# State space heads: logarithms of the time steps in the exponent, masks written by GpSimd

## The reference, cut to what matters

```python
def segsum_exp(a):                     # a = dt * A, T = 128
    cs = jnp.cumsum(a, axis=-1)
    diff = cs[..., :, None] - cs[..., None, :]
    tri = np.tril(np.ones((T, T), dtype=bool))
    return jnp.where(tri, jnp.exp(jnp.where(tri, diff, 0.0)), 0.0)
...
xdt = x * dt
CB = einsum('bclgn,bcsgn->bcgls', Cc, Bc)
Wd = CB * segsum_exp(adt)
y_diag = einsum('bcgrls,bcsgrp->bclgrp', Wd, xdt)
```

## Time and profile before

| | |
|---|---|
| median of 3 runs | 1833.98 us (1832.61 to 1834.04) |
| span of the profiled execution | 1831.0 us |
| PE busy | 1790.9 us, 98% |
| DVE busy | 1178.2 us, 64% |
| ACT busy | 846.6 us, 46% |
| POOL busy | 261.3 us, 14% |

### The profile page before, as it was taken

How to read it: one execution, slowest core, us unless ns; L and a number is a source line. 1 busy time by engine, 2 the same in 40 slices (tenths; PEclk the granted TensorE clock), 3 DMA queues, 4 the chain that set the end, 5 groups by cost and what they waited for, 6 DMA issues and landing times.

```text
span 1831.0 us, 24789 instructions
## 1 busy us (share of the span) xinstructions
PE 1790.9 (98%) x9602; PEld 1451.8 (79%) x9602; DVE 1178.2 (64%) x1913; ACT 846.6 (46%) x1623; POOL 261.3 (14%) x324
## 2 busy tenths in 40 slices
PE   7999999999999989999999999999999999999998
PEld 7767898888888877878878786667788998888886
DVE  6356643233345788897888955677556358686858
ACT  5356533222224565564655644554435444342435
POOL 1402000000000035254352540000020000000000
PEclk9999999999999999999999999999999999999999
DMA  7211333322332443353443444233543241414121
GB/s 243 81 59 55 90 126 103 105 92 92 93 92 74 150 141 129 117 146 101 153 134 117 139 148 154 85 103 124 139 149 124 73 153 63 153 35 161 58 92 46
DMA packets 128388, 205.69 MB, mean 112 GB/s; under 512 B 26496, under 2 KB 58688, under 8 KB 127632
## 3 DMA queue, kind: packets, MB, share of 16 engines
q1 hardware_dynamic: 118944, 166.70, 28.6%
q0 software_dynamic: 8464, 34.93, 5.3%
q10 hardware_dynamic: 864, 2.49, 0.3%
HBM read 191.37 MB, written 12.71 MB: 111 GB/s over the span
## 4 chain that ended last, share of the span: by engine, by line
PE 70%; DVE 21%; ACT 4%; issue 4%; DMA 0%; POOL 0%; DVEq 0%; ACTq 0%
PE m L2145 13%; PE m L2147 13%; PE m L2146 13%; PE m L2156 5%; PE m L2158 5%; PE m L2157 5%; DVE lo L1395 4%; PE s L2308 3%; DVE X L1799 3%; PE m L2280 2%; PE m L2282 1%; PE m L2281 1%; PE m L2253 1%; PE m L2255 1%; PE m L2254 1%
## 5 line engine op out<-in xcount | busy, mean ns | idle before, releaser
L2145 PE MATMUL m<-hH,hi 128*128 128x512 f32 (+1 forms) x1392 | 530.7, 381 | 3.0 <-DVE hL L1425 1.5
L2147 PE MATMUL m<-hH,lo 128*128 128x512 f32 (+1 forms) x1392 | 509.0, 366 | 0.0
L2146 PE MATMUL m<-hL,hi 128*128 128x512 f32 (+1 forms) x1392 | 508.5, 365 | 0.0
L1395 DVE TENSOR_TENSOR lo<-raw,hi 128x1024 fp32r<-128x1024 f32 x267 | 332.7, 1257 | 160.7 <-ACT hi L914 160.3
L914 ACT ACTIVATE hi<-raw 128x1024 fp32r<-128x1024 f32 x267 | 276.4, 1050 | 177.9 <-PE m L2147 41.9
L2145 PEld LDWEIGHTS m<-hH,hi 128*128 128x128 f32 x1392 | 262.5, 189 | 49.8 <-issue 5.4
L2147 PEld LDWEIGHTS m<-hH,lo 128*128 128x128 f32 x1392 | 262.4, 189 | 43.4
L2146 PEld LDWEIGHTS m<-hL,hi 128*128 128x128 f32 x1392 | 262.9, 189 | 40.1 <-issue 1.0
L2156 PE MATMUL m<-hi,hH 128*128 128x512 f32 (+1 forms) x320 | 134.8, 421 | 1.7 <-DVE lo L1395 1.7
L2158 PE MATMUL m<-hi,hL 128*128 128x512 f32 (+1 forms) x320 | 122.1, 381 | 0.0
L2157 PE MATMUL m<-lo,hH 128*128 128x512 f32 (+1 forms) x320 | 121.9, 381 | 0.0
(11 more groups left out here) (331 smaller groups left out, 3005.6 us busy)
## 6 DMA issues: line engine op xcount, KB each, us to landing
raw<-in_w_in_dram SPq DMA_DIRECT2D x72, 512.0 KB, 3.7
hn<-scr_cs_dram POOLq DMA_DIRECT2D x32, 512.0 KB, 4.1
raw<-in_w_up_dram SPq DMA_DIRECT2D x32, 512.0 KB, 4.8
wq<-in_w_down_dram SPq DMA_DIRECT2D x24, 512.0 KB, 8.4
raw<-in_w_gate_dram SPq DMA_DIRECT2D x44, 256.0 KB, 2.9
raw<-in_w_up_dram SPq DMA_DIRECT2D x44, 256.0 KB, 3.2
raw<-in_w_down_dram SPq DMA_DIRECT2D x22, 512.0 KB, 3.9
raw<-in_w_in_dram SPq DMA_DIRECT2D x33, 256.0 KB, 3.1
```

The source lines that it names most:

```text
L1395: e.tensor_tensor(d, r, h.bitcast(F32), ALU.subtract).then_inc(s_lo, 1)
L2145: e.matmul(bank, wh[:, kk, c], h[:, k, q], start=k == 0, stop=False)
L2146: e.matmul(bank, wh[:, kk, c], l[:, k, q], start=False, stop=False)
L2147: x = e.matmul(bank, wl[:, kk, c], h[:, k, q], start=False, stop=k == kt - 1)
```

## The change

The factor dt moves into the exponent: dt * exp(cs[l] - cs[s]) = exp(cs[l] + (ln dt[s] - cs[s])). `LDT` is the logarithm of dt, floored at 1e-30, and `BIAS` = LDT - CS. The masks are no longer in CB; GpSimd writes -1e30 over the masked halves of the broadcast rows, in place in HN, with one affine_select for each direction. ACT takes eight exponentials of 128x128 for each head, with BIAS as a bias per partition, into HA (slot T) and HB (slot T+1); DVE adds the two and multiplies by CB once (slot T+3). The minimum at T+1, the four scalar-and-tensor steps of DVE and the scaled copies of ACT are gone. CBM is one plain copy of CB, and NCS is gone. The DMA of head h waits for the exponentials of head h-2 instead of the minimum.

```diff
# ACT, steps(g)
+                if g == x + 2:
+                    o.wait_ge(s_dtd, 2)
+                    e.activation(LDT[:, :, :], LDT[:, :, :], ACT.Ln).then_inc(s_ldt, 1)
...
-                    e.activation(NCS[:, :, :], CS[:, :, 0:32], ACT.Copy, scale=-1.0).then_inc(s_dta, 1)
# ACT, state_space(g)
-                for h in HD_AT[1].get(g, ()):
-                    o.wait_ge(s_cbl[h % 2], 16 * (h // 2 + 1))
-                    o.wait_ge(s_dta, 10)
-                    if h >= 2:
-                        o.wait_ge(s_hw, h - 1)
-                    cb = HN[h % 2]
-                    for c in range(4):
-                        k = slice(128 * c, 128 * c + 128)
-                        x = e.activation(HA[:, h % 2, k], cb[:, k], ACT.Identity, bias=NCS[:, c, h:h + 1])
-                    x.then_inc(s_hid, 1)
-                for h in HD_AT[3].get(g, ()):
-                    o.wait_ge(s_hmin, h + 1)
-                    e.activation(HB[:, h % 2, :], HB[:, h % 2, :], ACT.Exp).then_inc(*o.own())
-                    o.wait_ge(s_cbm, h // 4 + 1)
-                    for c in range(4):
-                        k = slice(128 * c, 128 * c + 128)
-                        x = e.activation(HA[:, h % 2, k], CBL[:, c, :], ACT.Copy, scale=DT[:, c, 32 + h:33 + h])
-                    x.then_inc(s_hexp, 1)
+                for d in range(2):
+                    for h in HD_AT[1 + d].get(g, ()):
+                        o.wait_ge(s_hm, 2 * h + d + 1)
+                        o.wait_ge(s_bias, 1)
+                        if h >= 2:
+                            if d == 0:
+                                o.wait_ge(s_hw, h - 1)
+                            else:
+                                o.wait_ge(s_hd, h - 1)
+                        to = (HA, HB)[d]
+                        for c in range(4):
+                            k = slice(128 * c, 128 * c + 128)
+                            x = e.activation(to[:, h % 2, k], HN[h % 2][:, 512 * d + 128 * c:512 * d + 128 * c + 128], ACT.Exp,
+                                             bias=BIAS[:, c, 32 * d + h:32 * d + h + 1])
+                        x.then_inc(s_hexp, 1)
# DVE, steps(g)
+                    e.tensor_scalar(LDT[:, :, :], DT[:, :, :], 1e-30, None, ALU.max).then_inc(*o.own())
+                    o.settle()
                     e.tensor_tensor(x, DT[:, :, :], mid(ALOG, 4), ALU.mult).then_inc(s_dtd, 1)
+                if g == x0 + 9:
+                    o.wait_ge(s_dta, 6)
+                    o.wait_ge(s_ldt, 1)
+                    e.tensor_tensor(BIAS[:, :, :], LDT[:, :, :], CS[:, :, :], ALU.subtract).then_inc(s_bias, 1)
# DVE, state_space(g)
-                    o.wait_ge(s_hexp, 4 * i)
                     o.wait_ge(s_hw, 4 * i)
-                    b4 = side[0][:, :].rearrange("p (c l) -> p c l", c=4)
-                    e.tensor_tensor(CBU[:, :, :], b4, mid(CST[:, C_TF:C_TF + 128], 4), ALU.mult).then_inc(*o.own())
-                    e.tensor_tensor(CBL[:, :, :], b4, mid(CST[:, C_TB:C_TB + 128], 4), ALU.mult).then_inc(s_cbm, 1)
+                    e.tensor_copy(CBM[:, :, :].rearrange("p c l -> p (c l)"), side[0][:, :]).then_inc(s_cbm, 1)
                 for h in HD_AT[4].get(g, ()):
-                    o.wait_ge(s_hexp, h + 1)
-                    o.settle()
-                    for c in range(4):
-                        k = slice(128 * c, 128 * c + 128)
-                        x = e.scalar_tensor_tensor(out=HA[:, h % 2, k], in0=CBU[:, c, :], scalar=DT[:, c, h:h + 1], in1=HA[:, h % 2, k],
-                                                   op0=ALU.mult, op1=ALU.add)
-                    x.then_inc(*o.own())
-                    o.settle()
-                    e.tensor_tensor(HB[:, h % 2, :], HA[:, h % 2, :], HB[:, h % 2, :], ALU.mult).then_inc(s_hw, 1)
-                for h in HD_AT[2].get(g, ()):
-                    o.wait_ge(s_hid, h + 1)
-                    o.wait_ge(s_hib, h + 1)
-                    e.tensor_tensor(HB[:, h % 2, :], HA[:, h % 2, :], HB[:, h % 2, :], ALU.min).then_inc(s_hmin, 1)
+                    o.wait_ge(s_hexp, 2 * h + 2)
+                    e.tensor_tensor(HB[:, h % 2, :], HA[:, h % 2, :], HB[:, h % 2, :], ALU.add).then_inc(*o.own())
+                    o.wait_ge(s_cbm, h // 4 + 1)
+                    o.settle()
+                    e.tensor_tensor(HB[:, h % 2, :], HB[:, h % 2, :], CBM[:, :, :].rearrange("p c l -> p (c l)"), ALU.mult).then_inc(s_hw, 1)
# POOL, state_space(g)
                 for h in HB_AT.get(g, ()):
                     o.wait_ge(s_cbl[h % 2], 16 * (h // 2 + 1))
-                    o.wait_ge(s_dta, 6)
-                    if h >= 2:
-                        o.wait_ge(s_hd, h - 1)
-                    d = HB[:, h % 2, :].rearrange("p (c l) -> p c l", c=4)
-                    src = HN[h % 2][:, 512:1024].rearrange("p (c l) -> p c l", c=4)
-                    e.tensor_tensor(d, src, bc(CS[:, :, 32 + h], 128), ALU.subtract).then_inc(s_hib, 1)
+                    for d, sign in enumerate((1, -1)):
+                        x = HN[h % 2][:, 512 * d:512 * d + 512].rearrange("p (c l) -> p c l", c=4)
+                        e.affine_select(out=x, in_=x, pattern=[[0, 4], [sign, 128]], compare_op=ALU.is_ge, fill=NEG, base=0,
+                                        channel_multiplier=-sign).then_inc(s_hm, 1)
                 for h in HD_AT[0].get(g, ()):
                     if h >= 2:
-                        o.wait_ge(s_hmin, h - 1)
+                        o.wait_ge(s_hexp, 2 * h - 2)
                     e.dma_start(HN[h % 2][:, :], scr["cs"][h].partition_broadcast(128)).then_inc(s_cbl[h % 2], 16)
```

More of the change, by code:

```diff
@@ L522, in build @@
         s_dtc, s_dtt, s_dtx, s_dtp, s_dta, s_dtd, s_cs = (sem(f"s_{n}") for n in ("dtc", "dtt", "dtx", "dtp", "dta", "dtd", "cs"))
-        s_cb, s_cbm, s_hid, s_hib, s_hmin, s_hexp, s_hw, s_hd, s_y = (sem(f"s_{n}") for n in ("cb", "cbm", "hid", "hib", "hmin", "hexp", "hw", "hd", "y"))
+        s_cb, s_cbm, s_hm, s_hexp, s_hw, s_hd, s_y = (sem(f"s_{n}") for n in ("cb", "cbm", "hm", "hexp", "hw", "hd", "y"))
+        s_ldt, s_bias = sem("s_ldt"), sem("s_bias")
         s_cbl = [sem(f"s_cbl{i}") for i in range(2)]
@@ L572, in build @@
         ident = CST[:, C_ID:C_ID + 128]
-        NCS = CST[:, C_BT:C_BT + 128].rearrange("p (c h) -> p c h", c=4)
         DTB, ALOG, DSK = CST[:, C_BT + 128:C_BT + 192], CST[:, C_BT + 192:C_BT + 256], CST[:, C_BT + 256:C_BT + 288]
@@ L626, in build @@
         OT = [sb(f"OT{i}", [128, 256], c=P3) for i in range(2)]
-        CBU, CBL = sb("CBU", [128, 4, 128], c=P3), sb("CBL", [128, 4, 128], c=P3)
+        CBM = sb("CBM", [128, 4, 128], c=P3)
+        BIAS, LDT = sb("BIAS", [128, 4, 64], c=P3), sb("LDT", [128, 4, 64], c=P3)
         PREV = sb("PREV", [128, 2, 3, 256], c=P3)
@@ L1411, in norm_scale @@
                 if n >= 12:
-                    o.wait_ge(s_hmin, 32)
+                    o.wait_ge(s_hexp, 64)
                 o.settle()
@@ L1725, in steps @@
                 if g == x0 + 13:
-                    o.wait_ge(s_dta, 12)
+                    o.wait_ge(s_dta, 11)
                     e.tensor_tensor(WST[:, :, :], WST[:, :, :], DT[:, :, :], ALU.mult).then_inc(s_dtd, 1)
```

## The result

The median of five runs after the change is 1827.18 us (1825.61 to 1829.52), against 1833.98 us before. The ratio is 0.9966, with a 95% interval of 0.9954 to 0.9977: 6.8 us faster.

What follows compares the result with a forecast made beforehand. PE is the bound and only its 12.5 us of waits for DVE can be won. 10.8 us back, less 0.6 for the Ln and 1.2 for handoffs, nets 9.0: span 1822.0, plus 3.0 gives 1825.0 us; range 1821 to 1837.

Steps and rivals of the forecast that it cites:

- The OT waits in the heads: PE's waits for DVE's OT while heads run, 3 x 1.39 = 4.2 us: all gone.
- those for the states and gates: PE's waits on DVE for the states' OT, 1.0 us, and the gates, 0.5 us: gone.
- the three of 0.27: PE's three OT waits outside the heads, 0.8 us in all: stay, since no head work is in front.
- The product of a head ... Gone.: PE's five waits for DVE's head product, 4.3 us, right behind four multiply-adds: all gone.
- lo: PE's wait for DVE's lo, 1.7 us, where two conversions and the first head meet: 0.8 gone, 0.9 stays.
- the Ln: One more Ln on ACT at slot 394 with two table loads, 3.0 us; delays the copy of the sums by 0.6.
- -63.4 us on VectorE: DVE loses 58.7 us of multiply-adds and 5.5 of masked copies, gains 0.8 for LDT's maximum and BIAS.
- -20 us on ScalarE, and the ping-pong: ACT swaps 101.3 us for 81.2 of exponentials; ACT, DVE, ACT, DVE, with 56.5 us waiting, becomes POOL, ACT, DVE.
- +28.8 us on POOL at 1.04 a mask: POOL gains 64 masks, 66.6 us at the subtraction's price, and loses 32 subtractions, 37.8 us.
- POOL becomes the bound: Rival, chance 0.15: masks from about 1.5 us each make POOL the limit; at 1.9 us, time 1849.
- the ring: POOL's loop per head: DMA issue, both masks, last exponentials, next issue; 6.7 us against 7.1 for a head.
- The waits only change their name: Rival, chance 0.22: POOL's extra 28.8 us delays DVE's weight remainders and ACT; only 2.7 us won, 1831.3.

Runs made afterwards that it cites:

- late issue: Changed kernel with POOL's DMA issue of the next head's rows one slot later, behind the masks of the head before; 1820.91 us, ratio 0.9925.
- no multiply-adds: Kernel before the change with its four multiply-adds a head left out and nothing else changed; 1820.15 us, ratio 0.9924.
- tripled masks: Changed kernel with each affine_select done three times in a row; 1871.87 us, ratio 1.0210.
- late Ln: Changed kernel with the Ln of LDT moved from its own slot to behind ScalarE's copy of the sums; 1827.12 us, ratio 0.9963.

## Why the prediction was right, and where it was not

The direction, its size class and its mechanism were right; 1825.0 was forecast and 1827.2 measured, 2.2 us less won. That it came so near is in part luck: VectorE was relieved of far less than forecast (377 us busy between 600 and 1100 us, not near 347), and the waits went all the same.

- *VectorE is the bound behind TensorE's waits, and the multiply-adds are the load.* Right, and shown alone: they are worth 12.6 us of the stretch. That is close to the ceiling of 12.5 read from the waits, and no kernel here shortens the stretch by more than 12.7.
- *The OT waits in the heads, 4.2, and those for the states and gates, 1.5, go; the three of 0.27 stay.* All right.
- *"The product of a head ... Gone."* This is the step that failed: 2.3 of 4.3 us are left, 1.95 of them in one wait in group 0. *lo*: 0.9 was to stay, 1.6 did. Together 3.0 too little, against 0.4 too much in the costs (1.0 in three waits for XW where 1.2 was taken, 0.4 for the Ln where 0.6 was): 12.5 - 6.1 = 6.4 us of waits gone instead of 9.0. I looked at what stood ahead of the product on VectorE and not at what ran beside it on POOL, and when. I had named the queue (POOL's issue waits for the exponentials) and judged only the issue itself, not the masks behind it.
- *-63.4 us on VectorE.* (That is 2.0 us a head; the 1.8 written beside it are the multiply-adds alone.) 38.7 came. The term of 58.7 was sized by a mean that held 21.6 us of POOL's delay, and I counted that delay as leaving with its instructions. Taken out alone, they gave 39.0. With that term the sum is 39.0 + 5.5 - 0.8 = 43.7; the rest of 5.0 I put down to what the masks add over the subtraction that they replace, where they stand. With the late issue VectorE is busy 1131.6 us, 46.6 less than before.
- *-20 us on ScalarE, and the ping-pong.* 80.7 us for the 256 exponentials against 81.2 forecast, so the lines of the heads lost the 20. ScalarE's busy time in the whole run fell by 12.6 only: the Ln and the two more table loads of 1.28 (17 in place of 15) are 3.0 of the rest, and 5.0 I have not traced. What was said of the ping-pong decides nothing: without it (late issue) or with it (no multiply-adds), the stretch is 461.6 and 461.7 us.
- *+28.8 us on POOL at 1.04 a mask.* 17.9 in the whole run (0.86 a mask in the mean, of which 0.65 its own). The estimate from the subtraction was too dear. The 769 ns of the Trainium skill (GPSIMD Engine Reference, section Elementwise — side-by-side cycle accounting) lie between the median of 647 and the mean of 883, so the mask's own price is below them; undisturbed, a pair takes 1.22 us, 0.61 a mask.
- *The Ln.* The copy of the sums was to be 0.6 us late. It starts at 642.31 after and 640.44 before, and 1.32 of that is the later start of this execution (608.18 against 606.86): 0.55. Right, but worth nothing. Timeline of ACT in the changed kernel, the place of the earlier trace rows:

```profile
635.20 1.28 ACT L1144 ACT_TABLE_LOAD   x1
636.99 0.42 ACT L1144 ACTIVATE LDT<-LDT 128x256 f32<-128x256 f32 x1 [0.51 <-DVE X L1723]
...
639.53 1.28 ACT L1184 ACT_TABLE_LOAD   x1
640.82 0.63 ACT L1184 ACTIVATE X<-X 128x512 f32<-128x512 f32 x1
...
642.31 1.04 ACT L1148 ACTIVATE X<-s 32x512 f32<-32x512 f32 x2
```

The load starts in idle time, ahead of the wait of its Ln, as assumed; behind the second the tanh begins at once. The drain of 1.38 us of which the Trainium skill (ScalarE: Activation LUTs, section What ACT_TABLE_LOAD costs) speaks is in neither place (ScalarE's work ahead of the two loads ends 0.02 us before them), and the measured row decides.

- *POOL becomes the bound.* Not at the mask's real price. The tripled masks show that a slower case of this kind exists, by way of XW and not of the ring. *The waits only change their name:* a part of this came true, one that is tied to a place: with the issue moved the change wins 12.7 us of the stretch instead of 6.8.

One caution on sums of waits. From the kernel before to the one with the late issue, PE's waits fall from 12.5 to 2.7, by 9.8 us, and the stretch falls by 12.7. The records of matmuls around a stall are drawn longer (0.70 us in the rows above, 0.60 for the same pair without a wait, at 802.65 us with the late issue), so a wait is worth some 0.2 to 0.3 us more than its row says (the one of 0.42 us on XW at 820 us cost 0.65, by the distance of the products around it); the distance between two marks is the safer reading. My use of 12.5 as a ceiling came out right partly by luck: of the waits counted in it 2.3 us never left (0.8 for OT, 0.6 for lo and 0.9 for the product are still there with the late issue).

## What to carry to other kernels

On an engine with one queue, look behind each instruction that waits: ready work queued there starts when the awaited engine finishes, which is just when others start too. Moving one issue behind the masks was worth 5.8 us, nearly as much as the change itself. And when instructions on VectorE are priced for removal, use their median, without GpSimd's delay: 128 x 0.347 = 44.4 us would have been much nearer to the 39.0 that came than the 58.7 were. The delay stays, and falls on the instructions that come next.

## What was not expected of the hardware

- affine_select of 128x512 in float32, in place, takes 624 ns at least and 647 in the median, close to POOL's product of two times 256 elements (603), and less than the 1040 of a subtraction of two times 512.
- The program has two starts. The matmuls of 256 columns from 13.6 us on follow each other by 0.12 us in some executions, and by 0.21 up to about 17 us in others. Timeline of PE in the kernel before and after:

```profile
13.78 0.39 PE L2145 MATMUL m<-hH,hi 128*128 128x256 f32 x1 [1.54 <-DVE hL L1425]
...
14.47 0.28 PE L2147 MATMUL m<-hH,lo 128*128 128x256 f32 x1
14.59 0.28 PE L2145 MATMUL m<-hH,hi 128*128 128x256 f32 x1
```

```profile
14.87 0.41 PE L2141 MATMUL m<-hH,lo 128*128 128x256 f32 x1
15.09 0.41 PE L2139 MATMUL m<-hH,hi 128*128 128x256 f32 x1
```

The windows print a clock of 1.00 for both, but that says nothing for the second. The trace's first record of the clock, 1.00, stands at 12.0 us in the kernel before, ahead of these matmuls, and at 17.1 in the changed one, behind them. The kernel with the multiply-adds put back has a record for the slow pace. Its matmuls follow by 0.12 us up to 14.7 and then by 0.21, and the window of these reads 0.50, the lower level of 1.2 GHz:

```profile
14.90:18.00 3.10, 3.10 (x16) 3.10 (x16) 3.00 (x6) 3.07 (x6) 0.00 (x0) 0.50 1.01 399
```

So the late start is one in which the upper level comes later, or is lost again. It is no property of the change (the changed kernel with the late Ln and nothing else has the early start), and here it moves everything behind by 1.3 us. The first mark stands at 606.6 to 606.9 us where the first record of the clock lies at 11.4 to 12.9, and at 608.0 to 608.6 where it lies at 16.9 to 17.9 or the clock fell again. That is why the spans of the two profiled executions differ by 5.7 us where the medians differ by 6.8. The changed kernel's execution took 1827.18 us with a span of 1825.3, 1.9 more, so of the 3.0 us that the prediction added, some 1.1 were probably this. What decides when the upper level comes is open.
